# A transformer layer on one core: the relative-bias table made first, in sixteen copies, with its write and skewed read at other places of ScalarE's program

## The reference

```
proj   = x @ W_in + b_in      # q, k, v | indexer q, k, head weights | conv in | two gates
score  = sum_h w[t,h] * relu(qi[t,h] . ki[s]), causal;   sel = the 64 best keys of each query
logits = q . k / 8 + rel_bias[bucket(t - s)]             # 8 heads, T5 buckets, 32 of them
y_attn = softmax(logits over sel) @ v @ W_o_attn
y_conv = swish(LN(causal depthwise conv of width 31 over GLU)) @ W_o_conv
x1     = LN(alpha * x + (sigmoid(g1) * y_attn + sigmoid(g2) * y_conv) @ W_out)
h      = alpha * x1 + top-4-of-32 clamped SwiGLU experts(x1)
out    = LN(h + sigmoid(h @ W_pg) * (p @ W_pp))
```

## Time and profile before

| | us |
|---|---|
| median of 3 runs | 1220.11 |
| lowest, highest | 1216.22, 1221.19 |
| profiled execution, its own time | 1219.21 |
| its span, first to last instruction | 1217.5 |

### The profile page before, as it was taken

How to read it: one execution, slowest core, us unless ns; L and a number is a source line. 1 busy time by engine, 2 the same in 40 slices (tenths; PEclk the granted TensorE clock), 3 DMA queues, 4 the chain that set the end, 5 groups by cost and what they waited for, 6 DMA issues and landing times.

```text
span 1217.5 us, 13661 instructions
## 1 busy us (share of the span) xinstructions
PE 1156.0 (95%) x5604; PEld 581.2 (48%) x5604; DVE 294.6 (24%) x760; ACT 172.1 (14%) x331; POOL 11.1 (1%) x26
## 2 busy tenths in 40 slices
PE   7499999989999999999999799999999999999997
PEld 5388888853343434344344334434343443434346
DVE  0056964322111111212110211111111121111125
ACT  1014122011111101111010111111011111111112
POOL 0020000000000000000000000000000000000000
PEclk9799999989999999999997899999999999999999
DMA  9796438579999999999999989999999999999980
GB/s 313 157 343 199 139 140 335 196 292 430 427 428 428 426 429 427 427 428 429 426 426 426 391 311 406 428 426 427 427 429 427 429 426 428 425 427 429 428 355 36
DMA packets 64736, 448.16 MB, mean 368 GB/s; under 512 B 6968, under 2 KB 35928, under 8 KB 39832
## 3 DMA queue, kind: packets, MB, share of 16 engines
q1 hardware_dynamic: 58352, 440.84, 87.9%
q10 hardware_dynamic: 6312, 6.32, 2.2%
HBM read 444.53 MB, written 2.62 MB: 367 GB/s over the span
## 4 chain that ended last, share of the span: by engine, by line
PE 85%; DMA 7%; DVE 5%; issue 1%; ACT 1%; SPq 0%; ACTq 0%; DVEq 0%
PE bank L377 55%; PE bank L637 9%; PE bank L364 5%; DMA ring<-in_w_gu 3%; PE bank L397 3%; DMA bias_table<-arena 3%; PE bank L764 2%; PE bank L1040 2%; PE bank L778 2%; PE bank L384 2%; PE bank L692 1%; DVE arena L423 1%; PE bank L371 1%; DVE arena L417 1%; ACT arena L1203 1%
## 5 line engine op out<-in xcount | busy, mean ns | idle before, releaser
L377 PE MATMUL bank<-ring,arena 128*64 128x512 f32 x1712 | 380.6, 597 | 11.8 <-issue 6.8
L377 PE MATMUL bank<-arena 128*64 128x512 f32 x1456 | 323.6, 599 | 4.5 <-DVE arena L423 3.8
L377 PEld LDWEIGHTS bank<-ring,arena 128*64 128x64 f32 x1712 | 120.9, 137 | 249.5 <-issue 234.5
L377 PEld LDWEIGHTS bank<-arena 128*64 128x64 f32 x1456 | 102.2, 138 | 208.4 <-issue 194.8
L417 DVE TENSOR_TENSOR arena<-bank,arena 128x512 f32<-128x512 f32 x33 | 22.8, 692 | 618.2 <-PE bank L384 618.2
L637 PE MATMUL bank<-arena,ring 128*128 128x256 f32 x576 | 128.4, 384 | 7.5 <-DMA ring<-in_w_in 7.5
L637 PEld LDWEIGHTS bank<-arena,ring 128*128 128x128 f32 x576 | 110.1, 193 | 24.1 <-issue 9.2
L1203 ACT ACTIVATE arena<-bank 128x512 f32<-128x512 f32 x62 | 37.0, 597 | 398.5 <-PE bank L377 398.5
L397 PE MATMUL bank<-arena 64*128 64x512 f32 x272 | 67.6, 615 | 2.0 <-ACT arena L1206 1.4
L364 PEld LDWEIGHTS bank<-arena 128*128 128x128 f32 x512 | 63.1, 201 | 11.8 <-issue 11.4
L364 PE MATMUL bank<-arena 128*128 128x128 f32 x512 | 66.2, 289 | 0.3 <-DVE arena L450 0.3
(11 more groups left out here) (187 smaller groups left out, 527.6 us busy)
## 6 DMA issues: line engine op xcount, KB each, us to landing
ring<-in_w_gu SPq DMA_DIRECT2D x70, 2048.0 KB, 25.5
arena<-in_w_gu SPq DMA_DIRECT2D x58, 2048.0 KB, 26.3
ring<-in_w_dn SPq DMA_DIRECT2D x35, 2048.0 KB, 24.4
arena<-in_w_dn SPq DMA_DIRECT2D x29, 2048.0 KB, 26.4
ring<-in_w_in SPq DMA_DIRECT2D x19, 1024.0 KB, 14.9
ring<-in_w_out SPq DMA_DIRECT2D x4, 1024.0 KB, 5.2
arena<-in_w_pg SPq DMA_DIRECT2D x2, 2048.0 KB, 44.2
ring<-in_w_oa SPq DMA_DIRECT2D x2, 1024.0 KB, 5.6
```

Of the source, the lines that this page charges most:

```text
L377: mm = pe.matmul(to[half * CAP:(half + 1) * CAP, :], rows, w[:, half * 512:(half + 1) * 512], start=first, stop=last)
```

## The change

The table is computed by TensorE's first matmul, ahead of `two(0)`, and for all 128 partitions: `relb_copies` holds the 8 columns of `relb_sb` sixteen times side by side (a new copy on VectorE, its first instruction, with a new semaphore), so the matmul's output has 16 copies of the 8 table rows. ScalarE takes it out of the bank before its first evacuation. After two evacuations it issues the write to DRAM, now from 128 partitions, each of which supplies 8 of the 1024 pieces; the other two evacuations of `qiT` follow. The wait for the write and the two skewed reads stand in the relu loop, in front of the fifth relu. `wiT`, which shared its place with `tab_sb`, moves to another one. The layout of the table in DRAM stays the same.

```diff
--- before.py
+++ after.py
@@ -141,7 +141,7 @@
         qiT = view(EX + 4096, 1024).rearrange("p (a t) -> p a t", a=4)
         attnT = view(EX + 4096, 1024).rearrange("p (a t) -> p a t", a=4)
         kiT = view(EX + 5120, 256)
-        wiT = view(EX + 19840, 256)
+        wiT = view(EX + 19456, 256)
 
         def wiT_at(t):
             return wiT[:, t * P:(t + 1) * P]
@@ -157,8 +157,11 @@
         merged = view(EX + 12288, 2048).rearrange("p (a t) -> p a t", a=KD)
         xT_sb = view(EX + 14336, 2048).rearrange("p (k t) -> p k t", k=KD)
         bias = view(EX + 16384, 3072).rearrange("p (h s) -> p h s", h=H)
+
+        NC = P // H
         oneh_sb = view(EX + 19456, S + P)[0:NB, :]
-        tab_sb = view(EX + 19840, S + P)[0:H, :]
+        tab_sb = view(EX + 19840, S + P)
+        relb_copies = view(EX + 20224, P)[0:NB, :]
 
         o = EX + 5 * PAIR
         ident, upper, ones = view(o, P), view(o + 2 * P, P), view(o + 3 * P, P)
@@ -212,7 +215,7 @@
         small_in, late_in = sem("small_in"), sem("late_in")
         xT_in, x_in = [sem("xT_in0"), sem("xT_in1")], sem("x_in")
         first_in = [sem("first_in0"), sem("first_in1")]
-        relb_in = sem("relb_in")
+        relb_in, relb_copied = sem("relb_in"), sem("relb_copied")
         tab_out, bias_in, ln_in = sem("tab_out"), sem("bias_in"), sem("ln_in")
         bias_masked = sem("bias_masked")
         consts = sem("consts")
@@ -639,11 +642,11 @@
                         mm.then_inc(tile_done, 1)
                         tiles.up()
 
+                pe.wait_ge(relb_in, 32)
+                pe.wait_ge(relb_copied, 1)
+                pe.matmul(bank[7][:, 0:S + P], relb_copies, oneh_sb[:, :], start=True, stop=True).then_inc(tab_done, 1)
                 two(0)
                 two(1)
-
-                pe.wait_ge(relb_in, 32)
-                pe.matmul(bank[7][0:H, 0:S + P], relb_sb[:, :], oneh_sb[:, :], start=True, stop=True).then_inc(tab_done, 1)
 
                 wait_chunk(pe, 2)
                 w = w_view(2)
@@ -1105,13 +1108,15 @@
                     a.activation(dst, bank[n % 4][:, 0:S], func, bias=bias, scale=scale).then_inc(tile_out, 1)
                     cnt.up()
 
-                for j in range(4):
+                a.wait_ge(tab_done, 1)
+                a.activation(tab_sb, bank[7][:, 0:S + P], ACT.Identity).then_inc(tab_ready, 1)
+                for j in range(2):
                     evac(qiT[:, j, :], ACT.Identity, bT_sb[:, j:j + 1])
-                a.wait_ge(tab_done, 1)
-                a.activation(tab_sb[:, :], bank[7][0:H, 0:S + P], ACT.Identity).then_inc(tab_ready, 1)
                 a.wait_ge(tab_ready, 1)
-                a.dma_start(table.rearrange("q h i -> h q i"), tab_sb.unsqueeze(1).to_broadcast([H, P, S + P])
-                            ).then_inc(tab_out, 16)
+                a.dma_start(table.rearrange("(r c) h i -> (c h) r i", c=NC),
+                            tab_sb.unsqueeze(1).to_broadcast([P, P // NC, S + P])).then_inc(tab_out, 16)
+                for j in range(2, 4):
+                    evac(qiT[:, j, :], ACT.Identity, bT_sb[:, j:j + 1])
                 a.wait_ge(wi_done, 1)
                 for t in range(NT):
                     a.activation(wiT_at(t)[64:72, :], bank[6][64:72, t * P:(t + 1) * P], ACT.Identity).then_inc(wiT_out, 1)
@@ -1121,12 +1126,13 @@
                 a.wait_ge(bq_ready, 1)
                 for j in range(2):
                     evac(qT[:, j, :], ACT.Identity, bq[:, j:j + 1], 0.125)
-                a.wait_ge(tab_out, 16)
-
-                for lo, n, at in ((0, P, 2 * P - 1), (P, S, P - 1)):
-                    skew = bass.AP(tensor=table.tensor, offset=at, ap=[[H * (S + P) - 1, P], [S + P, H], [1, n]])
-                    a.dma_start(bias[:, :, lo:lo + n], skew).then_inc(bias_in, 16)
                 for h in range(H):
+                    if h == 4:
+                        a.wait_ge(tab_out, 16)
+
+                        for lo, n, at in ((0, P, 2 * P - 1), (P, S, P - 1)):
+                            skew = bass.AP(tensor=table.tensor, offset=at, ap=[[H * (S + P) - 1, P], [S + P, H], [1, n]])
+                            a.dma_start(bias[:, :, lo:lo + n], skew).then_inc(bias_in, 16)
                     a.wait_ge(dots_done, h + 1)
                     if h >= 2:
                         a.wait_ge(relu_used, 2 * h - 2)
@@ -1300,6 +1306,9 @@
             @block.vector
             def _(v):
                 c = Tally()
+                v.wait_ge(relb_in, 32)
+                nc.vector.tensor_copy(relb_copies.rearrange("b (c h) -> b c h", h=H),
+                                      relb_sb[:, :].unsqueeze(1).to_broadcast([NB, NC, H])).then_inc(relb_copied, 1)
                 v.wait_ge(small_in, 16 * 4)
                 nc.vector.tensor_scalar(bq, bT_sb[:, 4:8], 0.125, None, ALU.mult).then_inc(bq_ready, 1)
                 v.wait_ge(wi_done, 2)
```

## The result

| | us |
|---|---|
| changed kernel, median of 4 runs | 1201.70 (1200.87 to 1202.39) |
| kernel before, median of 4 runs | 1220.65 (1216.22 to 1222.91) |
| ratio, 95% interval | 0.9849 (0.982 to 0.9878) |
| profiled execution, its own time and span | 1200.87, 1199.1 |

Faster by 19 us. The forecast was 1200.7 in 1197 to 1207. The first lines of the new file push the rest down: L637 of before is L640 now, L672 is L675, L1133 is L1139. In the experiments' kernels the numbers differ from these by a few more lines.

A forecast was written before the change was run, and what follows sets the result against it. TensorE bounds the kernel, idling while ScalarE's relus wait behind the table's slow write to DRAM. Gains 17.07 + 1.59 + 0.33 + 0.5 - 0.1 = 19.4 us gave a forecast of 1200.7, range 1197 to 1207.

The forecast's parts named there:

- The idle: TensorE's wait before dots(4) for ScalarE's relus, held behind the table's write, goes away: 17.07 us gained.
- The products after the idle: dots(4), dots(6) and the next 64 matmuls no longer run slowly after the idle: 1.59 and 0.33 us gained.
- The table matmul at the front: Moved ahead of two(0), it leaves the path behind two(1), saving 0.73 and costing 0.2: net gain 0.5 us.
- The write: Table's write to DRAM issued at about 17 instead of 24.58, fast packets, sharing with weights, lasting 7.5 us.
- Its cost for chunk 3: Weight chunk 3, sharing the queues with the write, lands between 24.7 and 26.9; TensorE stalls 0.1 us (0 to 0.4).
- The two reads: Skewed reads issued by ScalarE at about 37 land at 52, hidden before GpSimd needs them at 60.
- the hole that I counted as cover: TensorE's idle before chunk 0's second half, expected to hide nearly all of the moved table matmul, leaving 0.2 us cost.
- the terms' bound downwards: How far the summed terms could push the time down: 0.6 us, used for the likeliest case's range, 1198 to 1204.
- A: Rival: a table packet costs an engine 206 ns wherever it comes from; 1201 to 1210, middle 1206; chance 0.07.
- B: Rival: the write still runs on 8 engines at 50 GB/s, only earlier, delaying weight chunks; 1211 us; chance 0.03.
- C: Rival: DRAM takes the write's pattern at 50 GB/s in total, over all 16 engines; 1222.7 us; chance 0.02.
- D: Rival: the gain at the logits is eaten in the experts by the weight stream's pace; 1220 us; chance 0.03.

The follow-up runs named there:

- the four-copy kernel: Changed kernel with the write's source cut to four copies on 32 neighbouring partitions, all else kept: 1201.37 us (6 runs), after a single execution of 1197.15.
- experiments 1 to 3: Kernel before, only wait and reads moved: 1214.71 us; changed kernel, all places put back, sixteen copies kept: 1202.17; changed kernel, one copy on 8 partitions: 1209.12.

## Why the prediction was right, by its own steps

*The idle, 17.07 us: right.* The hole in front of L675 is gone and no other took its place up to the logits.

*The products after the idle, 1.59 + 0.33: right.* dots(4) and dots(6) take 44.57 - 43.05 = 1.52 against 3.10; the next 64 matmuls take 58.48 - 44.57 = 13.91 against 77.86 - 63.54 = 14.32 before, 0.41 gained where I had 0.33.

*The table matmul at the front, net 0.5: half of it.* The copy is 0.21 us where I had 0.4, the matmul starts at 6.18 and takes 1.61, as worked out. (That 128 rows cost no more than 8 is not quite so: behind two(1) the matmul took 0.81 with 8 rows, 0.83 with 32 and 0.91 with 128.) But the small chunk's product starts at 23.77 instead of 23.96, and two(3) at 27.23 instead of 27.48: 0.25 net. The cost at the front was 0.5, not 0.2: the hole that I counted as cover closed, yet two(1) ends at 7.73 + 16.21 = 23.94 instead of 10.97 + 12.32 = 23.29.

*The write: right in place, time and sharing.* Issued at 17.07 (17), packets at 65 ns (79 or below), most of it between 21 and 28, one for one with the weights. It was a little faster than worked out, since both queues together moved 388 to 396 GB/s in its stretches of 2 us where I had 349. *Its cost for chunk 3, 0.1: none.* The chunk landed at 24.8, inside the 24.7 to 26.9 that I had, and was wanted at 27.2.

*The two reads: right.* Issued at 37.33, 16.3 us to the landing of the longer one, at 54; I had 14.8 and 52. GpSimd's additions begin at 61.18, behind the top-k and not behind the reads.

Sum up to the logits: 17.07 + 1.58 + 0.41 + 0.25 = 19.3; the logits start at 79.30 instead of 98.67, 19.37 earlier. The forecast's 19.4 is that near by luck in the small terms: 0.25 too much for the table's matmul, 0.1 and 0.07 too little for chunk 3 and the products. The 0.6 that I gave as the terms' bound downwards does not follow either; 0.2 + 0.1 = 0.3 does. The profiled executions differ by 1219.21 - 1200.87 = 18.3. The missing 1 us lies behind the logits and is no wait: the second routing product takes 3.46 us in place of 1.93, and some 0.5 us comes back in the experts. I had put what lies behind the logits at nothing. The granted clock of the routing's 10.4 us is 0.73 where it was 0.84:

```profile
222.30:232.70 10.40, 8.21 (x53) 7.60 (x51) 6.05 (x22) 4.00 (x7) 0.77 (x2) 0.73 1.01 429
```
```profile
241.60:252.00 10.40, 7.86 (x68) 7.12 (x65) 6.96 (x28) 4.00 (x7) 0.77 (x2) 0.84 1.00 427
```

(The first is the changed kernel, the second the kernel before.) The engine has short matmuls and waits there, and whether it falls to the lower level differs between executions of one program: the four-copy kernel had 1.93 once and 3.46 at another time. Of the eleven profiled executions only that one and the kernel before had 1.93, the others 2.99 to 3.47, so these traces do not exclude that the earlier start makes the slow one more frequent.

Of the rivals, A, B and C were each made real or excluded: B costs 7.4 us against the changed kernel (1209.12 against 1201.70; I had 1211), A next to nothing, and C is excluded, since the same table went to DRAM at 95 and at 240 GB/s, and at 118 in the old order of its pieces. D did not happen: the first expert's matmuls stand 17.8 us earlier and the end 18.3. That loads wait for TensorE and not the reverse was read rightly.

The reasons were weaker than the number in one point. I gave the idle's removal to two parts of the change together. The runs separate them: the source's spread gives 19 us alone, the moved wait 7 alone, and they do not add.

## What to carry to other kernels

A DMA whose source is a few neighbouring partitions, read over and over, can be several times slower than its bytes suggest (50 against 240 GB/s here), and it slows the other queue on the engines it occupies. A destination of that form, and a source read only once, were not tried. Look at its time per packet; before moving waits around it, spread the rows: 32 neighbours or rows four partitions apart were enough here. Where a wait is moved down its engine's program, look for what is queued behind its new place: here the idle came back one chunk later, 10.5 us of 17.

## What the runs showed of the hardware that I had not expected

- With reads from DRAM and writes to it at the same time, the two queues moved 388 to 396 GB/s, where reads of 1 KB pieces alone had 349. The store's pieces are also larger (1.5 KB), and no run separates the two. In 24 to 26 us of the changed kernel the store moved 240 GB/s and the loads 160, so it cost them some 190.
- A single copy on 8 engines with rows four apart moved 118 GB/s beside the weights, more than the 95 GB/s of twice as many engines on neighbours.
- One program's times spread over up to 7.6 us (ten runs of the kernel before, beside experiments 1 to 3), and where traces of it can be compared, TensorE's clock in the routing and in one expert is where they part.
